# State space heads: outputs in two runs of four heads, and two of eight heads' differences on ScalarE

## The reference, cut to what matters

```python
a_cum = jnp.cumsum(log_a, axis=-1)
seg = a_cum[..., :, None] - a_cum[..., None, :]
decay_in = jnp.exp(jnp.where(causal, seg, -jnp.inf))
cb = jnp.einsum("bclgn,bcsgn->bcgls", cc, bc)
y_diag = jnp.einsum("bcgjls,bcsgjp->bclgjp", cb[:, :, :, None] * decay_in, x_)
...
y_off = jnp.einsum("bclgn,bcgjpn,bcgjl->bclgjp", cc, prev, jnp.exp(a_cum))
return (y_diag + y_off).reshape(b, s, h, p)
```

## Time and profile before

| | us |
|---|---|
| median of 3 runs | 1702.16 (1702.12 to 1702.25) |
| the profiled execution | 1701.79, span 1700.0 |
| TensorE busy | 1688.2 (99%) |
| VectorE busy | 1141.7 (67%) |
| ScalarE busy | 814.1 (48%) |
| granted TensorE clock, mean | 0.998 |

### The profile page before, as it was taken

How to read it: one execution, slowest core, us unless ns; L and a number is a source line. 1 busy time by engine, 2 the same in 40 slices (tenths; PEclk the granted TensorE clock), 3 DMA queues, 4 the chain that set the end, 5 groups by cost and what they waited for, 6 DMA issues and landing times.

```text
span 1700.0 us, 22047 instructions
## 1 busy us (share of the span) xinstructions
PE 1688.2 (99%) x8742; PEld 1392.8 (82%) x8742; DVE 1141.7 (67%) x1687; ACT 814.1 (48%) x1167; POOL 30.7 (2%) x57
## 2 busy tenths in 40 slices
PE   9999999999999999999999999999999999999998
PEld 7888888878887888888888888888888888888886
DVE  7754346878886645677776344667888777878574
ACT  6223234765756323322222334666667577665522
POOL 0000000000000000000000000100000000000000
PEclk9999999999999999999999999999999999999999
DMA  5234232333332222332233333542222222222332
GB/s 208 96 99 127 99 100 89 122 100 104 120 105 82 96 92 98 99 99 91 95 100 99 103 107 112 202 145 77 86 78 84 75 87 75 88 86 76 118 105 87
DMA packets 50550, 174.82 MB, mean 103 GB/s; under 512 B 5872, under 2 KB 8048, under 8 KB 50320
## 3 DMA queue, kind: packets, MB, share of 16 engines
q1 hardware_dynamic: 45200, 155.45, 27.7%
q0 software_dynamic: 5248, 17.96, 3.3%
HBM read 164.93 MB, written 4.26 MB: 100 GB/s over the span
## 4 chain that ended last, share of the span: by engine, by line
PE 98%; DMA 1%; DVE 1%; ACT 0%; issue 0%; SPq 0%; DVEq 0%; ACTq 0%
PE bank L582 83%; PE bank L688 4%; PE bank L602 2%; PE bank L882 2%; PE bank L798 1%; PE bank L894 1%; PE bank L796 1%; PE bank L756 1%; DMA raw<-stream 0%; PE bank L908 0%; PE bank L667 0%; PE bank L920 0%; PE bank L777 0%; DVE X L2250 0%; PE bank L922 0%; PE bank L924 0%
## 5 line engine op out<-in xcount | busy, mean ns | idle before, releaser
L582 PE MATMUL bank<-u_high,w_high 128*128 128x512 f32 x1504 | 592.1, 394 | 0.0
L582 PE MATMUL bank<-u_high,w_low 128*128 128x512 f32 x1504 | 585.8, 389 | 0.0
L582 PE MATMUL bank<-u_low,w_high 128*128 128x512 f32 x1504 | 585.1, 389 | 0.0
L993 ACT ACTIVATE w_high<-raw 128x1024 fp32r<-128x1024 f32 x283 | 298.9, 1057 | 573.5 <-PE bank L582 559.8
L1567 DVE TENSOR_TENSOR w_low<-raw,w_high 128x1024 fp32r<-128x1024 f32 x282 | 344.7, 1223 | 253.5 <-ACT w_high L993 247.8
L582 PEld LDWEIGHTS bank<-u_high,w_high 128*128 128x128 f32 x1504 | 282.4, 188 | 59.6 <-issue 2.7
L582 PEld LDWEIGHTS bank<-u_high,w_low 128*128 128x128 f32 x1504 | 282.3, 188 | 59.6
L582 PEld LDWEIGHTS bank<-u_low,w_high 128*128 128x128 f32 x1504 | 282.6, 188 | 57.9 <-issue 1.0
L1658 DVE TENSOR_TENSOR h_raw<-bank,rs 128x512 f32<-128x512 f32 x44 | 30.4, 691 | 61.8 <-PE bank L582 55.0
L582 PE MATMUL bank<-f_high,w_high 128*128 128x512 f32 x176 | 68.5, 389 | 0.0
L582 PE MATMUL bank<-f_low,w_high 128*128 128x512 f32 x176 | 68.5, 389 | 0.0
(11 more groups left out here) (393 smaller groups left out, 2497.3 us busy)
## 6 DMA issues: line engine op xcount, KB each, us to landing
raw<-stream SPq DMA_DIRECT2D x283, 512.0 KB, 3.3
rows<-running POOLq DMA_DIRECT2D x32, 256.0 KB, 3.5
X<-x_t SPq DMA_DIRECT2D x8, 256.0 KB, 4.8
residual<-X POOLq DMA_DIRECT2D x4, 512.0 KB, 4.7
u_high<-n_high_rows POOLq DMA_DIRECT2D x4, 512.0 KB, 8.4
u_low<-n_low_rows POOLq DMA_DIRECT2D x4, 512.0 KB, 9.5
X<-residual POOLq DMA_DIRECT2D x4, 512.0 KB, 5.4
masks_f<-masks SPq DMA_DIRECT2D x1, 1280.0 KB, 6.0
```

The source lines that it names most:

```text
L582: ins = pe.matmul(acc[:], w[:, k], x[:, at + k], start=start and k == first and j == 0, stop=stop and k == KT - 1 and j == 2)
L993: act.activation(w_high[:, n % HI_RING], raw[:, n % RAW_RING], ACT.Copy).then_inc(hi_done, 1)
```

## The change: what it does

Pair runs 0 and 1 both follow block 12, pair runs 2 and 3 both follow block 16. Products of heads 4, 5 move from step 14 to 15; their exponentials from 13 to 14. Differences of heads 6, 7 move from 11-13 to 14 (those of 2, 3 stay at 9, of 4, 5 at 13, as the table gives them). `take_y` comes for two pairs at once at steps 13 and 17, `group_square` and `add_square` a step later; in the last group, where step 18 is past the loop, squares and sums of pairs 2 and 3 stand behind the loop. For heads 3 and 7 of each group, VectorE's `differences` is left out, and ScalarE makes it as four Relu of 128x128 (relu(column - row)), with the following exponential scaled by -1. ScalarE waits once for `d_tok` before the zone, and POOL's load of the next row of such a head waits for its second exponential.

```diff
-TAKE = {11: 0, 13: 1, 15: 2, 17: 3}
+TAKE = {13: (0, 1), 17: (2, 3)}
+
+MIN_AT = {7: (0, 1), 9: (2, 3), 13: (4, 5), 14: (6, 7)}
+EXP_AT = {9: (0, 1), 11: (2, 3), 14: (4, 5), 15: (6, 7)}
+INTO_AT = {10: (0, 1), 12: (2, 3), 15: (4, 5), 16: (6, 7)}
+
+BY_SCALAR = (3, 7)
+
+
+def mins_until(n):
+
+    return sum(k % 8 not in BY_SCALAR for k in range(n + 1))
...
-                if i in (10, 12, 14, 16):
-                    heads_y(g, (i - 10) // 2)
+                if i in (12, 16):
+                    heads_y(g, (i - 12) // 2)
+                    heads_y(g, (i - 12) // 2 + 1)
...
+            act.wait_ge(d_tok, 1)
...
-                act.wait_ge(s_min, n + 1)
-                act.activation(seg[h % 4][:], seg[h % 4][:], ACT.Exp).then_inc(s_exp, 1)
+                if h in BY_SCALAR:
+                    for c in range(NCH):
+                        cs = slice(c * P, (c + 1) * P)
+                        ins = act.activation(seg[h % 4][:, cs], rows_of[n % 4][:, cs], ACT.Relu, scale=-1.0, bias=tok[:, 1, c, n:n + 1])
+                    link(ins)
+                else:
+                    act.wait_ge(s_min, mins_until(n))
+                act.activation(seg[h % 4][:], seg[h % 4][:], ACT.Exp, scale=-1.0 if h in BY_SCALAR else 1.0).then_inc(s_exp, 1)
...
-                if i - 1 in TAKE:
-                    group_square(g, TAKE[i - 1])
+                for j in TAKE.get(i - 1, ()):
+                    group_square(g, j)
...
-                if i in (9, 11, 13, 15):
-                    head_exp(g, i - 9)
-                    head_exp(g, i - 8)
+                for h in EXP_AT.get(i, ()):
+                    head_exp(g, h)
...
+            group_square(GROUPS - 1, 2)
             group_square(GROUPS - 1, 3)
...
-                    if i in (10, 12, 14, 16):
-                        for h in (i - 10, i - 9):
-                            into_c(g, h)
-                            into_cb(g, h)
+                    for h in INTO_AT.get(i, ()):
+                        into_c(g, h)
+                        into_cb(g, h)
...
-                    if i in (7, 9, 11, 13):
-                        differences(g, i - 7)
-                        differences(g, i - 6)
+                    for h in MIN_AT.get(i, ()):
+                        if h not in BY_SCALAR:
+                            differences(g, h)
...
-                    if i in TAKE:
-                        take_y(g, TAKE[i])
-                    if i - 1 in TAKE and TAKE[i - 1]:
-                        add_square(g, TAKE[i - 1])
+                    for j in TAKE.get(i, ()):
+                        take_y(g, j)
+                    for j in TAKE.get(i - 1, ()):
+                        if j:
+                            add_square(g, j)
...
+            add_square(last, 2)
             add_square(last, 3)
...
-                    pool.wait_ge(s_exp, 2 * (n - 4) + 1)
-                    pool.wait_ge(s_min, n - 4 + 1)
+                    pool.wait_ge(s_exp, 2 * (n - 4) + (2 if (n - 4) % 8 in BY_SCALAR else 1))
+                    pool.wait_ge(s_min, mins_until(n - 4))
```

More of the change, by code:

```diff
@@ L1219, in _ @@
                         if j == 6:
-                            act.wait_ge(s_min, HEADS - 3)
+                            act.wait_ge(s_min, mins_until(HEADS - 4))
                         evac(("gate_s", j), sig_s[j][:], ACT.Sigmoid)
@@ L1250, in _ @@
                         cast_y(k)
-                    act.wait_ge(s_min, HEADS - 2)
+                    act.wait_ge(s_min, mins_until(HEADS - 3))
                     evac(("gate_s", KT - 1), sig_s[KT - 1][:], ACT.Sigmoid)
```

## The result

The changed kernel takes 1704.48 us (median of 20 runs, 1703.12 to 1705.46), the kernel before 1702.20 (20 runs, 1701.35 to 1702.75). One execution of the kernel before, timed beside e5 to e7, ran at a mean granted clock of 0.752 and took 2118.8 us; this slow run is in none of the ratios.

The account below looks back on a forecast made before the run. TensorE, busy 99%, was taken as the bound. Seams -2.6, middle waits +1.7, bank +2.5, split rows +0.1 give +1.7 us on 1701.79, so 1703.5; with 0.37 to the median, 1703.9 us, range 1700.8 to 1705.9.

Parts of the forecast that it names:

- the sum as forecast: Whole kernel: all terms together give +1.7 us; a time within 1702.5 to 1705.2 us had chance 0.62.
- Both named waits: TensorE waits for late products before pair run 3, 1.7 us in sum, and for gate_s 2's bank, 2.5 us.
- the seams: Pair runs merged on TensorE: a run right behind another costs 1.56 us, a gain of 2.6 us in all.
- the rival by which the seams give nothing: Merged pair runs: each keeps its own gaps, 2.6 us of gain go, 1705.8 us; chance 0.07.
- run 2 saves less where the b run stays: Step 14 of all groups but the last: merging run 2 gains 0.26 us in place of 0.36.
- Run 3 in the middle groups: Second and third group: late products make TensorE wait 0.8 us each before pair run 3; first group 0.1.
- The price of a Relu: ScalarE's Relu for heads 3 and 7: 0.29 us for each next one, four 1.27; upper case 0.4 each.
- The bank of gate_s 2: Last group, step 14: ScalarE empties this bank late, TensorE waits 2.5 us at block gate_s 5; bounds 2.2 and 2.9.
- The rival of a load with a drain: ScalarE's path to emptying gate_s 2: two table switches with drains add 2.7 us, 1706.6 us; chance 0.01.
- The covers: Other delayed work, such as run 1's products and x tiles, costs nothing; one more add_square behind the zone costs 0.1 us.

Follow-up runs that it names:

- e5: e3 with the banks of gate_s 2 and 3 emptied between the exponentials of heads 4 and 5 in the last group's step 14: 1701.23 us, ratio 0.9993.
- e7: e3 with head 5 of the last group also getting its difference from four Relu on ScalarE: 1705.57 us, ratio 1.0017.
- e4: The changed kernel with the edits of e1 and e3 together: 1699.42 us, ratio 0.9983.
- e2: The changed kernel with all eight differences on VectorE again, no Relu on ScalarE: 1702.91 us, ratio 1.0003.
- e3: The changed kernel with the next group's copy Btok made ahead of the exponentials of heads 6 and 7 at step 15: 1702.42 us, ratio 1.0001.
- e1: The changed kernel with the banks of gate_s 2 and 3 emptied at the head of the last group's step 14: 1701.08 us, ratio 0.9991.
- e6: e4 with all eight differences on VectorE, no Relu on ScalarE: 1699.56 us, ratio 0.9984.

## Why the prediction was right, point by point

The forecast was 1703.9 us, the median is 1704.5; the sum was +1.7 us, measured +2.3, inside the 1702.5 to 1705.2 of the sum as forecast. Both named waits and the seams are as forecast. That nearness owes something to chance all the same: one term was missing (1.6 us, in the traced execution and probably in 12 of 20), and the seams gave 0.2 us more than was taken.

- **The seams**: forecast a gain of 2.6 us. Right. e4, which has nothing but the seams, is 2.8 us faster than 1702.2. The seam was taken as 0.02 us and is 0; the rival by which the seams give nothing falls. That run 2 saves less where the b run stays also held: from run 1 to run 3 e4 is 0.27 us shorter than before in the second group (forecast 0.26) and 0.37 in the last (forecast 0.36). Another 0.1 us came back behind run 3 in the second group, which the forecast did not have.
- **Run 3 in the middle groups**: forecast waits of 0.8, 0.8 and 0.1 us, by the chain two squares, table loads, exponentials, Relu, Btok, CBm, norm row, products. Measured 0.7, 0.7 and none. The step from the product's end to TensorE was taken as 0.2 and is 0.15 (404.07 to 404.22). e2 (without the Relu) and e3 (Btok first) each shorten this chain at one place, and either suffices. The price of a Relu was bounded between 0.29 and 0.4: four last 1.27 us, as the working from the earlier trace rows gave them.
- **The bank of gate_s 2**: forecast 2.5 us. The wait itself was right (2.4 in the gap, 2.5 with the 0.1 by which the second matmul behind it is late), and the steps to it too, shown here in ScalarE's timeline of the changed kernel beside the earlier trace rows:

```profile
520.84 1.06 ACT L1007 ACTIVATE w_high<-raw 128x1024 fp32r<-128x1024 f32 x1 [7.86 <-PE bank L595]
...
522.95 1.28 ACT L1132 ACT_TABLE_LOAD   x1
...
526.46 1.28 ACT L1015 ACT_TABLE_LOAD   x1
527.75 1.08 ACT L1015 ACTIVATE sig_s<-bank 128x512 f32<-128x512 f32 x2
```

  From w_high to the emptying 6.91 us, forecast 6.92, and the emptying starts 1.29 us behind the start of its table load. The rival of a load with a drain, from the Trainium skill ("ScalarE: Activation LUTs", "What ACT_TABLE_LOAD costs"), is not borne out by these rows.
- **What was missing**: the term is the same one, "2.2 to 2.9, by the latency and a drain more or less"; it prices the wait and takes what comes behind it as nothing. The wait had 3.4 us at half clock behind it, 1.6 us more, in the traced execution and, by clock and time, probably in 12 of 20. In the stream of before nothing showed it, for the longest wait there, 1.0 us, has none behind it. Only the end of that trace hinted at it: the last matmul ends at 1692.4, and from 1694.4 on the granted clock stands at half, with TensorE idle for 2.0 us. e1 took the stretch away with the wait, e5 with half of the wait.
- **The covers**: right. The x tiles were in time (the last xdec row ends at 417.59, `new_states` starts at 418.64 there), and one `add_square` more behind the zone shows as less than 0.1 us. For run 1 of the second group there was more cover than forecast: its products end at 372.69, 4.2 us ahead of it, forecast 2.6. That VectorE has no `differences` at step 11 any more, as the forecast says, is because those of heads 4 and 5 move too, from step 11 to 13; the description of the change has them staying at 13.
- That relu belongs on VectorE is a rule of the Trainium skill ("ScalarE: Activation LUTs", "Rules for kernel authors"). Here e4 and e6, with and without the Relu, differ by 0.14 us, inside the scatter. In the changed order the Relu cost 1.4 to 1.6 us (e2's two waits), by standing ahead of a copy for which another engine's queue stopped: e3 keeps them and loses both waits.

## What to carry to other kernels

When work is moved in a queue that also empties the banks of a full stream, add up what now stands ahead of each emptying; two instructions in the wrong place cost 4.1 us here, and eight merged runs gave 2.8. A wait of TensorE is priced by the gap in its starts, not by the waits view (0.7 for 0.5, 2.4 for 2.2), and a long one also by the stretch at half clock that can follow it. Where a margin is used up, try first to put the short instruction that others wait for ahead of the rest of its step: here that took away both kinds of wait, and nothing else came late for it (e4).

## What the runs showed of the hardware

- TensorE's granted clock stayed at 2.4 GHz behind gaps of 1.3 us (e5) and fell to 1.2 GHz for 3.4 us behind gaps of 2.4 us (changed kernel, e2, e3) and 3.7 us (e7), in each of these traces. Where it falls differs: in e3 it is low from the first matmul behind the gap on, in the others it falls 0.7 to 1.0 us after TensorE has gone on (by the granted clock in the windows). At the end of the program, where TensorE stops for good, it fell 2.0 to 4.2 us behind the end of the last matmul, in all nine traces.
- It is not the same in every execution: the runs of kernels with a gap of 2.4 us or more scatter over 2.3 to 3.7 us, those of e1, e4, e5 and e6 over 1.1 to 1.8. The scatter alone is no proof of it, for the kernel before, without such a gap, scatters over 1.4 us in 20 runs, 2.2 in 33 and 2.7 in 26. In e7 the runs lie up to 3.5 us apart, more than one stretch costs, and six of the 11 have a mean clock of 0.997; whether they had two stretches was not traced.
- Two pair runs behind each other have no seam, though the second waits for semaphores of its own: satisfied waits in TensorE's queue cost nothing there (1.58 us from start to start for 14 steps, 1.54 added in all).
